# Angles of a state-space table reduced in one pass, half of its input tables built by GpSimd, and layer 0's scan placed later and worked in place

## What is computed

```
h = rmsnorm(x);  u, sq, sk, sv, dq, dk, dv, gate_logits = split(h @ w_in)
y_ssm: dt = exp(log_dt); lam_bar = exp(lam * dt); b_bar = (lam_bar - 1) / lam * b      (complex)
       states = associative_scan over the sequence of (lam_bar, b_bar @ u)
       y = c_re @ states.real - c_im @ states.imag + d * u;  glu(gelu(y) @ w_glu)
y_sb = stick-breaking attention(sq, sk, sv);  y_da = differential attention(rope(dq), rope(dk), dv)
x += sum(sigmoid(gate_logits) * (each branch @ w_branch)) @ w_out
x += cross attention(rmsnorm(x), rmsnorm(mem));  x += relu(rmsnorm(x) @ w_up)**2 @ w_down
```

## Time and profile before

| | |
|---|---|
| time, median of 3 runs | 1093.74 us (1093.61 to 1093.97) |
| profiled execution | 1096.48 us, of which the trace's span is 1094.8 us |
| mean granted clock of TensorE | 0.985 of full speed |
| TensorE busy | 1029.5 us, 94% |
| VectorE, ScalarE, GpSimd busy | 736.7 us (67%), 573.4 us (52%), 176.7 us (16%) |
| HBM traffic | 161 GB/s over the span |

### The profile page before, as it was taken

How to read it: one execution, slowest core, us unless ns; L and a number is a source line. 1 busy time by engine, 2 the same in 40 slices (tenths; PEclk the granted TensorE clock), 3 DMA queues, 4 the chain that set the end, 5 groups by cost and what they waited for, 6 DMA issues and landing times. The chain is left out here.

```text
span 1094.8 us, 18335 instructions
## 1 busy us (share of the span) xinstructions
PE 1029.5 (94%) x7096; PEld 937.9 (86%) x7096; DVE 736.7 (67%) x1061; ACT 573.4 (52%) x868; POOL 176.7 (16%) x304
## 2 busy tenths in 40 slices
PE   5778999999999899999989999999999989999996
PEld 4766889989998799988979878998998979899995
DVE  4884975878875565887465579478787647555554
ACT  6446445546765555546554454554637546444442
POOL 5993300000000003997000011000000000000000
PEclk9889999999999999999999999999999999999998
DMA  7253336645554366654556543465565445666661
GB/s 281 97 173 95 98 120 194 201 141 174 176 175 149 96 232 182 189 172 136 172 173 189 163 130 97 135 213 154 155 181 175 146 135 160 190 189 192 182 188 74
DMA packets 58022, 177.21 MB, mean 162 GB/s; under 512 B 14160, under 2 KB 16208, under 8 KB 57680
## 3 DMA queue, kind: packets, MB, share of 16 engines
q1 hardware_dynamic: 57792, 176.04, 52.2%
q10 hardware_dynamic: 144, 0.00, 0.0%
HBM read 172.87 MB, written 3.15 MB: 161 GB/s over the span
## 5 line engine op out<-in xcount | busy, mean ns | idle before, releaser
L1295 DVE TENSOR_TENSOR s_w_lo<-s_raw,s_w_hi 128x1024 fp32r<-128x1024 f32 x312 | 377.3, 1238 | 146.7 <-ACT s_w_hi L898 143.0
L898 ACT ACTIVATE s_w_hi<-s_raw 128x1024 fp32r<-128x1024 f32 x312 | 321.0, 1054 | 215.2 <-PE p_T L1821 130.5
L1819 PE MATMUL p_T<-s_hT_hi,s_w_hi 128*128 128x256 f32 x1088 | 313.4, 288 | 12.0 <-DVE s_w_lo L1295 11.9
L1820 PE MATMUL p_T<-s_hT_lo,s_w_hi 128*128 128x256 f32 x1088 | 310.0, 285 | 0.0
L1821 PE MATMUL p_T<-s_hT_hi,s_w_lo 128*128 128x256 f32 x1088 | 309.7, 285 | 0.0
L1819 PEld LDWEIGHTS p_T<-s_hT_hi,s_w_hi 128*128 128x128 f32 x1088 | 210.7, 194 | 17.6 <-issue 16.2
L1820 PEld LDWEIGHTS p_T<-s_hT_lo,s_w_hi 128*128 128x128 f32 x1088 | 210.8, 194 | 0.4
L1821 PEld LDWEIGHTS p_T<-s_hT_hi,s_w_lo 128*128 128x128 f32 x1088 | 210.9, 194 | 0.0
L1819 PE MATMUL p_A<-s_w_hi,s_bT_hi 128*128 128x512 f32 x320 | 125.2, 391 | 2.4 <-DVE s_bT_lo L1295 2.4
L1820 PE MATMUL p_A<-s_w_lo,s_bT_hi 128*128 128x512 f32 x320 | 124.7, 390 | 0.0
L1821 PE MATMUL p_A<-s_w_hi,s_bT_lo 128*128 128x512 f32 x320 | 124.6, 389 | 0.0
(11 more groups left out here) (263 smaller groups left out, 1685.5 us busy)
## 6 DMA issues: line engine op xcount, KB each, us to landing
s_raw<-in_weights SPq DMA_DIRECT2D x312, 512.0 KB, 3.6
s_bt<-in_mem_t SPq DMA_DIRECT2D x2, 1024.0 KB, 6.1
s_st_y<-in_x_t SPq DMA_DIRECT2D x2, 512.0 KB, 6.9
s_x<-in_x SPq DMA_DIRECT2D x1, 1024.0 KB, 10.6
s_vN<-in_ssm_bc SPq DMA_DIRECT2D x2, 512.0 KB, 8.9
u_turn<-s_st_y SPq DMA_DIRECT2D x4, 256.0 KB, 3.8
s_uB<-u_turn SPq DMA_DIRECT2D x8, 128.0 KB, 3.4
s_bt<-in_mem SPq DMA_DIRECT2D x1, 1024.0 KB, 5.9
```

Of the source, the lines that this page charges most:

```text
L898: return nc.scalar.activation(o, i, f, **kw)
L1295: return V.tensor_tensor(o, i0, i1, op)
L1819: mm(o, lhi, rhi, start=first, stop=False, **kw)
L1820: mm(o, lhi, rlo, start=False, stop=False, **kw)
```

## The change

**Angles.** GpSimd makes all seven multiples of the angle in one operation, VectorE reduces them all at once (with the rope's angle as an eighth) and ScalarE takes one pass of absolute value, sine and cosine over them. GpSimd's table work has fewer and wider operations, in the powers as in the phase table, and `zero_b` comes before the powers.

**Input tables.** `p_cv` for r = 1 and both halves of `p_bv` go from VectorE to GpSimd, ahead of the phase table: per layer twelve operations, of `p_cv` two products and two sums of 768 columns, of `p_bv` four products and four sums of 1024 (each sum on 64 of the 128 rows). Their scratch lies in `s_bt`. VectorE keeps `p_cv` for r = 0 and `p_b0`. `p_ct` goes from ScalarE to VectorE. The first `p_bt` stages come one unit later.

**Start.** The statistics of the first norm go from unit -1 to unit 0; ScalarE prepares chunks 2 and 3 within the angle stages. VectorE's row and the evacuation of u come in unit 2. SyncE issues `turn_u` at chunks 14, 15 and 18.

**Layer 0's scan.** `ssm_in` is in units 11 to 14, `ssm_out` in 13 to 16, and what follows moves by two units. The states are worked in place in `s_st_y`, so that dv's evacuation no longer waits for them.

```diff
@@ side_stages
-    after(-1, "stats", "mix", 0)
-    after(-1, "stats", "mix", 1)
     if l == 0:
         after(-1, "p_angle", 0)
         after(-1, "p_cos", 0)
-        after(2, "lam", 0)
-        after(3, "lam", 1)
-        after(4, "p_params", 0)
-    after(1, "row")
+    for half in range(2):
+        after(-1 if l else 0, "stats", "mix", half)
+    if l == 0:
+        after(2, "u_out")
+        after(3, "lam_sum")
+        after(4, "lam_exp")
+        after(5, "lam")
+        after(13, "p_params", 0)
+    after(1 if l else 2, "row")
...
-        pre(0, dict(ct=0, cv=(1, 2), b0=3, bv=(4, 5), k=(5, 6), bt=(6, 7, 7, 8)))
+        pre(0, dict(ct=-1, cv=2, b0=4, k=(5, 6), bt=(7, 8, 9, 10)))
...
-        pre(1, dict(ct=up0 + 10, cv=(up0 + 12, up0 + 13), b0=up0 + 15, bv=(up0 + 16, up0 + 18),
+        pre(1, dict(ct=up0 + 10, cv=up0 + 12, b0=up0 + 14,
                     k=(up0 + 20, up0 + 21), bt=(up0 + 22, up0 + 23, up0 + 24, up0 + 25)))
...
-FIRST = [9, 9]
+FIRST = [11, 9]
-DVE_PREP_EARLY = set(range(0, 5)) | set(range(AT_UNIT["up", 0, 0], NU))
+DVE_PREP_EARLY = set(range(0, 6)) | set(range(AT_UNIT["up", 0, 0], NU))
-        states = gates[:, 0:8, :].rearrange("p (r i) n -> p r (i n)", r=2).rearrange("p r (i m) -> p r i m", m=NB)
+        states = st_y[:, :, :].rearrange("p r (i m) -> p r i m", m=NB)
@@ new helpers, called with the vector engine's or GpSimd's tt
+        def products(tt, raw, r, f, n, parts, made, st):
+            q = [o[:, 0:n * STILES * GC].rearrange("p (n i c) -> p n i c", n=n, c=GC) for o in parts]
+            tt(q[0], spread(raw[:, r, :, :], n), places(FACTORS[:, 0, f:f + n, :], n)).then_inc(*st.mid())
+            tt(q[1], spread(raw[:, 1 - r, :, :], n), places(FACTORS[:, 1, f:f + n, :], n)).then_inc(*st.mid())
+            made()
+            for h in range(2):
+                yield slice(STATES * h, STATES * h + STATES), h, q
+
+        def cv_products(tt, t, r, parts, made, st):
+            for rows, h, q in products(tt, c_raw, r, 0, BL - 1, parts, made, st):
+                o = ct[rows, r, :, :].rearrange("p i (n h c) -> p n i h c", n=BL, h=2)[:, 1:BL, :, h, :]
+                yield tt(o, q[0][rows], q[1][rows], ALU.subtract if r else ALU.add)
+
+        def b_products(tt, r, f, n, parts, out, made, st):
+            for rows, h, q in products(tt, b_raw, r, f, n, parts, made, st):
+                yield tt(out(rows, GC * h), q[0][rows], q[1][rows], ALU.add if r else ALU.subtract)
@@ SyncE's loop over the chunks c
-                    if c in (8, 10, 12):
-                        turn_u(l, c // 2 - 4, st)
+                    if c in (14, 15, 18):
+                        turn_u(l, (14, 15, 18).index(c), st)
@@ GpSimd, tables(t)
-                tt(TH[:, 1, :], TH[:, 0, :], const(5)[:, 0, :]).then_inc(*st.mid())
+                tt(TH[:, 1:1 + TAB_STEPS, :], TH[:, 0:1, :].broadcast_to([P, TAB_STEPS, STILES]),
+                   consts[:, 0:TAB_STEPS].unsqueeze(2).broadcast_to([P, TAB_STEPS, STILES]))\
+                    .then_inc(*st.sig(theta_ready, t + 1))
...
-                zero_b(st, t, l)
...
+                product(factor(3, 2), factor(5, 2), factor(1)).then_inc(*st.sig(pow_ready, t + 1))
+                pool.wait_ge(*st.mine())
+                pool.wait_ge(*st.at(ct0_ready, t + 1))
+                twice = [bt[:, 0, 8 * i:8 * i + 8, :].rearrange("p i n -> p (i n)") for i in range(2)]
+                for h, ins in enumerate(cv_products(tt, t, 1, twice, lambda: pool.wait_ge(*st.mine()), st)):
+                    ins.then_inc(*st.sig(ct_ready[1], t + 1)) if h else ins.then_inc(*st.mid())
+                for r in (1, 0):
+                    pool.wait_ge(*st.mine())
+                    for h, ins in enumerate(b_products(tt, r, 3, BL, twice,
+                                                       lambda rows, c: bN[rows, r, :, :, c:c + GC].rearrange("p i j c -> p j i c"),
+                                                       lambda: pool.wait_ge(*st.mine()), st)):
+                        ins.then_inc(*st.sig(bv_ready[r], t + 1)) if h else ins.then_inc(*st.mid())
...
+                    e, o = phase[:, :, :, 0:n], phase[:, :, :, n:2 * n]
+                    tt(o, e, c[0]).then_inc(*st.mid())
+                    tt(part, e, c[1]).then_inc(*st.mid())
@@ ScalarE
+                        if s in (("p_angle", 0), ("p_cos", 0)):
+                            prep_chunk(2 + (s[0] == "p_cos"))
+                            n_first = AHEAD
...
-                        if kind == "dv":
-                            act.wait_ge(*st.at(s_ready, KB))
                         if kind == "sv":
                             act.wait_ge(*st.at(diag_ready, NT))
+                            for r in range(2):
+                                act.wait_ge(*st.at(bv_ready[r], l + 1))
@@ VectorE
                 def p_cos(t):
-                    dve.wait_ge(*st.at(turn_ready, t + 1))
-                    V.tensor_scalar(THR, THR, PI_SAFE, -PI_SAFE, ALU.min, ALU.max).then_inc(*st.sig(angle_ready))
+                    n = angles(t)
+                    dve.wait_ge(*st.at(theta_ready, t + 1))
+                    reduce_angle(st, TH[:, 0:n, :], KK[:, 0:n, :], THR[:, 0:n, :])
+                    V.tensor_scalar(THR[:, 0:n, :], THR[:, 0:n, :], PI_SAFE, -PI_SAFE, ALU.min, ALU.max)\
+                     .then_inc(*st.sig(angle_ready))
...
+                def p_cv(t):
+                    dve.wait_ge(*st.at(pow_ready, t + 1))
+                    for h, ins in enumerate(cv_products(tt, t, 0, parts(t), lambda: dve.wait_ge(*st.mine()), st)):
+                        ins.then_inc(*st.sig(ct_ready[0])) if h else ins.then_inc(*st.mid())
...
-                def p_bv(t, r):
-                    times_b(t, r, 0, BL, lambda rows, c: bN[rows, r, :, :, c:c + GC].rearrange("p i j c -> p j i c"))\
-                        .then_inc(*st.sig(bv_ready))
```

## The result

The changed kernel takes 1114.34 us (median of 4 runs, 1111.06 to 1115.92) where the kernel before takes 1093.86 (median of 4): 1.0181 times as long, with a 95% interval of 1.0153 to 1.0209. The forecast was 1100 us with a range of 1081 to 1110. It was slower, as forecast, but by 20.5 us instead of 6.3, and outside the range. The profiled execution took 1115.91 us, its span is 1114.2 us and the mean granted clock 0.974 (before: 0.985).

The account below looks back on a forecast made before the run. TensorE was taken to bound the kernel nearly everywhere. Layer 0's -3, layer 1's +9.5 and 0 for the rest gave +6.5 us on the profiled 1096.48, 1103.0; less 2.74 for the median, rounded to 1100, range 1081 to 1110.

Parts of the forecast that it names:

- the lock is shorter than an instruction: Rival, chance 0.23: VectorE gets in within a microsecond whatever the width of GpSimd's operation; about -12 us, 1082.
- no contention: Rival, chance 0.08: the engines don't hinder each other, all early gaps but the attention's go, 24.6 us; 1069.
- Layer 1 hides it: Rival, chance 0.10: low parts of 445 to 480 us find slack in the MLP's units; sum near 0, 1093.
- GpSimd is dearer: Rival, chance 0.11: 2.5 us per 1024-column operation or dearer strided sums, 27 us per set; about 1111.
- The first gap: TensorE's wait for chunk 4, up to 29.75 us: 6.51 us and 1.8 of clock go, sq ends 8.3 earlier.
- 11.4 us of lateness: Layer 1's tables, 445 to 480 us: 49.4 us of shared work in 35, about 3 absorbed by VectorE's lead.
- half a microsecond of clock: Layer 1's tables: clock counted as coming back, since GpSimd's phase table is done in fewer operations.
- the alternation: Layer 1's tables: taking turns leaves each engine short moments without work, 1 to 2 us of loss.
- the time of 67.7 us: Layer 0: when VectorE finishes what it had done at 61 us, up to `p_b0` and chunk 13; 67 to 69.
- the sum of shared time: Layer 0: VectorE's 18.5 us plus GpSimd's 21.7, 40 us that can't overlap, from 28 or 29 us on.
- The two waits: Layer 0: TensorE stands still for chunk 10 (9 us) and for `p_b0` ahead of `p_k` (10 us).
- What costs nothing: Later transfers of u, layer 0's scan in place and the gelu three units later: 0, from -1 to +2 us.

Follow-up runs that it names:

- e1: The changed kernel with the second `p_cv` and both `p_bv` given back to VectorE in both layers, `p_b0` moved along: 1098.05 us, 1.0029 of the kernel before.
- e6: e1 with GpSimd's wide phase table operations and the copy of the decay cut into pieces of 256 columns: 1094.76 us, 0.9997 of the kernel before.
- e5: The changed kernel with GpSimd's input tables in pieces of 256 columns and the rope's angles moved behind the norm's low parts: 1092.34 us.
- e8: e7 with u's transfers issued at chunks 10, 12 and 16 instead of 14, 15 and 18: 1090.09 us, 0.9946 of the kernel before.
- e7: The changed kernel with input tables, phase table and decay copy in pieces of 256 columns, rope's angles behind the norm's low parts: 1090.91 us.

## Why the prediction was right or wrong

**Right in kind.** Slower was forecast, for the reason that the runs bear out: undoing the tables gives 16.3 us, and the width alone turns a ratio of 1.018 into 0.992. The rivals "the lock is shorter than an instruction" and "no contention" fell with the rows at 460 us. "Layer 1 hides it" fell with chunk 123. "GpSimd is dearer" came nearest in time (1111), but its reason didn't come: it wanted 2.5 us for each operation of 1024 columns.

**Right in size.** The first gap: 8.3 us forecast, chunk 5 is 8.9 us better off than chunk 0 was. GpSimd's operations of 1024 columns hold VectorE for 1.80 and 2.23 us, where 1.75 and 2.2 were put in. `pow_ready` comes at 28.9 us, as forecast, though the small tables took 6.3 us instead of 3 to 4 (they began earlier). Between 445 and 480 us 11.4 us of lateness were forecast; TensorE's waits there are 12.4 (1.4 and 11.06).

**What was off.** In the traces +6.5 us was forecast and 19.4 came; the miss is 6.3 us in layer 1 and 6.5 in layer 0.

In layer 1, +9.5 was forecast and 15.8 measured. The step that failed is "half a microsecond of clock" given back. The term for the clock should have been a loss: a wait of 11 us leaves TensorE at half speed behind it (0.50 through 477 to 482 us), and the next wait again (0.50 at 496 to 500). From chunk 121 to 123 the kernel loses 13.8 us for a wait of 11.1, and from 123 to 127 5.9 for one of 2.8: 5.8 us of clock. I had taken exactly this into account in layer 0 and left it out in layer 1. The second miss there is smaller: 1.4 and 2.8 us of further waits, where the text had 1 to 2 for the alternation. What the kernel before lost there and the changed one doesn't is 5.8 us (25.1 to 19.3), where I gave back 4.2. The sum itself was also added up too high: 11.4 less 4.2, plus 1 to 2, is 8.2 to 9.2 and not 9.5.

In layer 0, -3 was forecast and +3.5 measured. The step that failed is the time of 67.7 us for what VectorE had done at 61: it was 71.9, at the end of `p_b0`. A part of that was in the numbers already: 40.2 us from 28 or 29 us on end at 68.2 or 69.2, not at 67.7. The rest is that the sum of shared time stopped at the twelve operations; behind them GpSimd's phase table goes on, now in operations of 64 to 512 columns at that moment (16 to 64 before), and `p_b0` takes 6.2 us (65.67 to 71.90) where it took 4.1 (54.67 to 58.80). What the width of the phase table costs there isn't settled: from e1 to e6 chunk 12 moves by 0.7 us. The two waits came out as 13.3 and 5.6 us where 9 and 10 were forecast, so their sum was right and their shares were not. Unit 6 begins 4.8 us later than the 72.5 of the forecast:

```profile
77.25 0.80 PE L1779 MATMUL p_T<-s_w_hi,s_hT_hi 128*128 128x512 f32 x1
```

And unit 6, which was to run "at more clock than the 0.77 of before" and give back 2 us, ran at 0.50 up to 80 us, for the same reason as in layer 1, and gave back some 0.3 (an estimate: 3.3 us of it at half clock, after 4.1 before). These two are the 6.5 us between -3 and +3.5. The 2.3 us of the cast behind a memset, which the prediction had at nothing, lie ahead of these waits, and e5 shows that most of it is swallowed by the next wait.

**What costs nothing** held as far as it was tried: the transfers of u (e8, under 1 us), and from chunk 60 to 113 nothing moves. Between chunks 15 and 35, where scan and gelu were moved, the changed kernel makes up 2.4 us, as much as it no longer waits for the input tables (1.5) and waits less on the attention (3.1 to 2.2), so that part isn't a loss; whether it is a gain wasn't tried alone.

**The range** left out the case that came: it was built on the price of GpSimd's operations, whose lower ends proved right, and held no case for the clock behind new waits. Had it had one, 5.8 us of layer 1 and some 2 of layer 0, the forecast would have been 1108. Layer 1 came out inside its own ends (+2 to +18), layer 0 outside (-14 to +2).

**Open.** In layer 1 the waits (11.1, 2.8 and 1.4) and 5.8 us of clock, less the 5.8 that vanish, are 15.3 of the 15.8 us. Why 512 columns save only a quarter of what 256 do isn't settled, nor what the scan in place, `p_ct` on VectorE and the phase table's earlier place are worth by themselves.

## What to carry to other kernels

Before work is moved from VectorE to GpSimd, count VectorE's two-input operations that run beside it: each may wait for one whole GpSimd operation, so the price can be GpSimd's full time, not a share. If it is moved, cut it into short pieces, so that each of VectorE's operations waits for little: here 128 columns instead of 1024 turned a loss of 1.8% into a gain of 0.8%, and with 256 where the tables are urgent and three smaller edits it was 1.2%. And where a new wait of TensorE is forecast, add what it then loses at half clock: 5.8 us behind waits of 13.9 us here. That term has a spread of its own: behind the same 6.7 us the clock in 64 to 69 us was 0.97 in e8 and 0.62 in e7.

## What the runs showed of the hardware

- The exclusion goes by whole instructions and alternates: with both engines busy, operations of 1.23 and 1.80 us became 2.9 us each, and with GpSimd's at 128 columns VectorE's 1.23 us rose to 1.35 only.
- So narrow operations cost the other engine little and wait long themselves. In the kernel before, three GpSimd operations of 16 columns, 0.20 us each alone (0.40 for two at 25.24 us), take 3.26 us beside VectorE's tables, while VectorE's pair of low parts at 463.24 us takes 2.38, 1.2 each:

```profile
461.29 3.26 POOL L727 TENSOR_TENSOR s_small<-s_small 128x16 f32<-128x16 f32 x3
```

- It isn't limited to VectorE's two-input operations. A cast of 128x2 waited 2.4 us for a GpSimd memset (2.58 us instead of 0.18), while a two-input operation beside a memset doesn't. In the kernel before, the low part beside the same memset (3.92 to 7.43 us) takes its 1.23 us, and the pair at 450.58 us, with GpSimd clearing `s_gates` from 450.98 on, takes 2.36, 1.2 each:

```profile
6.10 1.23 DVE L1295 TENSOR_TENSOR s_w_lo<-s_raw,s_w_hi 128x1024 fp32r<-128x1024 f32 x1 [4.49 <-ACT s_w_hi L898]
...
450.58 2.36 DVE L1295 TENSOR_TENSOR s_w_lo<-s_raw,s_w_hi 128x1024 fp32r<-128x1024 f32 x2 [0.26 <-ACT s_w_hi L898]
```

  The Trainium skill's page "SBUF — State Buffer", section "Who interferes with whom", has both: casts and copies can, when their operands meet the conditions, run in modes that take both of VectorE's ports and then contend with GpSimd, while a tensor_tensor contends with a GpSimd instruction that reads, not with one that only writes. The traces agree with both effects; that this cast ran in such a mode no row shows.
